# Hybrid block, one core: compact norms, softplus sums in two fp32r passes, and mixer work moved between tiles

## Chip, core and metric

One core of a Trainium2 chip (TensorE, VectorE = DVE, ScalarE = ACT, GpSimd = POOL, SyncE = SP for the loads). The metric is the device time of one execution in microseconds, median of three runs.

## What is computed

One decoder layer, x of 256 tokens by 2048 features, fp32 throughout:

```python
proj = rms_norm(x, g1) @ w_in                    # 8 groups of 512 columns, 3 x 2048 gates
o_a = hgrn2_mixer(q, f, i, g)                    # gated linear recurrence, 4 heads of 128
o_b = s5_mixer(u)                                # complex diagonal state space, then GLU
o_c = stick_breaking_mixer(q, k, v)              # q, k normed per head
merged = sum(sigmoid(gate_k) * (o_k @ w_branch[k]) for k in range(3))
x = x + merged @ w_out
x = x + (silu(up_a) * up_b) @ w_down             # up = causal conv of rms_norm(x, g2) @ w_up
```

Branch A ends in `o * rsqrt(mean(o*o))` over each head's 128 features; branch C norms q and k the same way. Branch C also needs, per head, the sum of softplus(z) over all later keys:

```python
within = cumsum(log_keep, reverse=True) - log_keep       # log_keep = -softplus(z), masked
later = cumsum(blk_tot, reverse=True) - blk_tot          # of whole key blocks of 128
w = exp(log_sigmoid(z) + within + later)
```

## The kernel before

Everything is kept with features on the 128 partitions and the 256 tokens along the row. The big products go by output tiles of 128 features: 32 tiles for the 8 groups, 48 for the gates, then GLU, branches, `w_out`, `w_up`, `w_down`. A tile of `w_in` needs 16 blocks of 128x128 weights, in two pieces of 8. fp32 precision is had from fp32r operands (one pass each) by splitting weights and activations in a high and a low part and taking three products. So each piece is loaded by SP into one of 4 `raw` buffers, ScalarE copies it to `w_hi` (L689), VectorE writes `w_lo = raw - w_hi` (L999), and TensorE uses both: in `in_piece` (L356) as three matmuls of 256 columns per block, in `piece` (L342, L344) as one of 512 and one of 256. The ring of 4 pieces is two tiles: ScalarE may overwrite a piece once TensorE has used it, and loop step n of ScalarE and VectorE makes the pieces of tile n + 2.

All the small work of the branches is hung into the `w_in` loop, by a step number n. TensorE runs `mixers(n)` after tile n, ScalarE and VectorE run `mixers(n + 1)` in step n, behind their two pieces, so that what they do there goes on beside TensorE's tile n + 1. Each engine works in order: a long step delays the pieces that stand behind it. The order is written by hand in a table, `AT`, with `TABLE_AT` for the S5 cosine tables and `STATES_AT` for the S5 states:

```python
AT = {"norm1": 7, "s5_bT": 18, "hg_vT": 15, "hg_o": 30, "hg_ss": 31, "q_ss": 35, "k_ss": 35, "sb_vT": 36,
      "z0": 39, "z1": 39, "within0": 42, "within1": 42, "sb_o": 45}
AT.update({f"lev{k}": 12 + 2 * k for k in range(LEVELS + 1)})
STATES_AT = (43, 46, 51, 54, 59, 62, 67, 70)
```

The places that matter below:

- `lev1` to `lev8`: attention of branch A by levels. VectorE writes a level's factors (L1202, L1203), TensorE waits for them.
- The split of the normed input `a_in` (L1232), 16 blocks, four in each of steps 11 to 14; `s5_input_weights`, steps 16 and 17.
- `hg_ss`, `q_ss`, `k_ss`: the sums of squares, each as two full fp32 products of `ones` (128x128) with 512 columns, so that every row of the result is the sum (L401). Then VectorE takes the mean (L1050), ScalarE Ln and Exp, VectorE one Newton step, all on 128x1024, and multiplies.
- `z0`, `z1`: logits. ScalarE copies them out and makes log(1 + exp(-|z|)), VectorE the softplus `SOFTP` and log-sigmoid (128x1536), masks both; `within0`, `within1` sum them with the triangle `lower` and `ones` as fp32 products.
- The branch stage: VectorE's `gate_product` (L1415) multiplies a bank by its gate, GpSimd's `merge` adds three of them (L1580, L1582), ScalarE and VectorE split the sum (L894, L1406) for `w_out`. Before `merge`, GpSimd issues one load of the whole residual `x1`, 2 MB (L1570).

An fp32 matmul of the program is two records in the trace. Small fp32 products whose output is a strip of 32 rows (`s5_y`) or whose input is one (`bu`) are there already.

## Time and profile before

| | |
|---|---|
| median of 3 runs | 1419.68 us (1418.05 to 1420.31) |
| the profiled execution | 1416.86 us, span 1415.2 us |
| TensorE busy | 1401.0 us, 99% of the span |
| VectorE, ScalarE, GpSimd busy | 73%, 54%, 10% |
| chain that ended last | TensorE 84%, VectorE 8%, issue 3%, ScalarE 2% |
| mean granted TensorE clock | 0.998 |
| HBM | 184 GB/s over the span |

Busy time of TensorE is the union of its records; an idle gap of it is given with what ended it. The granted clock is 1.00 at 2.4 GHz and 0.50 at 1.2 GHz.

### The profile page before, as it was taken

The numbers are of one execution on the slowest core, as the hardware profiler recorded it, in microseconds if no ns is written. First come the engines' busy times: TensorE is split into PE (matmuls) and PEld (weight loads), VectorE is DVE, ScalarE is ACT, GpSimd is POOL, SyncE is SP. The second block draws the span as 40 slices with busy tenths as digits, with TensorE's granted clock in tenths as the row PEclk, the third lists the DMA queues.
The fourth block names the chain that finished last, engine by engine and source line by source line (L and its number), as shares of the span: only waits on it lengthen the run. The fifth ranks groups of instructions, "written<-read, shape, count | busy, mean of one in ns | idle before, by whom it ended". The sixth has DMA issues, their size and how long they took to land.

```text
span 1415.2 us, 27392 instructions
## 1 busy us (share of the span) xinstructions
PE 1401.0 (99%) x9654; PEld 1291.2 (91%) x9654; DVE 1036.5 (73%) x1412; ACT 764.4 (54%) x1058; POOL 136.7 (10%) x182
## 2 busy tenths in 40 slices
...
GB/s 291 184 171 165 164 149 153 145 179 178 147 182 177 184 190 217 204 190 192 164 208 194 192 179 194 191 191 190 182 191 192 184 193 182 204 196 193 196 205 112
DMA packets 75503, 261.66 MB, mean 185 GB/s; under 512 B 8688, under 2 KB 9232, under 8 KB 75312
## 3 DMA queue, kind: packets, MB, share of 16 engines
...
HBM read 258.66 MB, written 2.10 MB: 184 GB/s over the span
## 4 chain that ended last, share of the span: by engine, by line
PE 84%; DVE 8%; issue 3%; ACT 2%; POOL 1%; DMA 1%; SPq 0%; POOLq 0%; DVEq 0%; ACTq 0%
PE bank L342 38%; PE bank L356 22%; PE bank L344 20%; DVE w_lo L999 3%; PE pair L401 2%; PE bank L367 1%; POOL merged L1580 1%; ACT w_hi L689 1%; DMA raw<-w_br 1%; POOL merged L1582 1%; DVE tmp L1023 0%; DVE a_in L1232 0%; ACT gates L699 0%; DVE proj L1023 0%; DMA x_first<-xT 0%
## 5 line engine op out<-in xcount | busy, mean ns | idle before, releaser
L999 DVE TENSOR_TENSOR w_lo<-raw,w_hi 128x1024 fp32r<-128x1024 f32 x496 | 584.7, 1191 | 311.3 <-ACT w_hi L689 307.3
L689 ACT ACTIVATE w_hi<-raw 128x1024 fp32r<-128x1024 f32 x496 | 507.8, 1030 | 413.1 <-PE bank L344 200.7
L342 PE MATMUL bank<-h,w_hi 128*128 128x512 f32 x1408 | 488.4, 390 | 0.0
L344 PE MATMUL bank<-h,w_lo 128*128 128x256 f32 x1408 | 397.1, 282 | 0.0
L356 PE MATMUL bank<-a_in,w_hi 128*128 128x256 f32 x2048 | 367.3, 283 | 5.2 <-DVE w_lo L999 5.2
L356 PEld LDWEIGHTS bank<-a_in,w_hi 128*128 128x128 f32 x2048 | 314.1, 189 | 9.9 <-issue 6.9
L342 PEld LDWEIGHTS bank<-h,w_hi 128*128 128x128 f32 x1408 | 264.2, 188 | 55.4
L356 PE MATMUL bank<-a_in,w_lo 128*128 128x256 f32 x1024 | 286.7, 280 | 0.0
L344 PEld LDWEIGHTS bank<-h,w_lo 128*128 128x128 f32 x1408 | 266.1, 189 | 0.0
L342 PE MATMUL bank<-act,w_hi 128*128 128x512 f32 x660 | 228.8, 390 | 0.0
L356 PEld LDWEIGHTS bank<-a_in,w_lo 128*128 128x128 f32 x1024 | 194.1, 190 | 0.0
L344 PE MATMUL bank<-act,w_lo 128*128 128x256 f32 x660 | 186.1, 282 | 0.0
L342 PEld LDWEIGHTS bank<-act,w_hi 128*128 128x128 f32 x660 | 123.8, 188 | 26.0
L344 PEld LDWEIGHTS bank<-act,w_lo 128*128 128x128 f32 x660 | 124.7, 189 | 0.0
L1607 POOL TENSOR_TENSOR padded<-sum_u,rstd 128x256 f32<-128x256 f32 x88 | 73.7, 838 | 413.3 <-DVE sum_u L1020 400.5
L342 PE MATMUL bank<-a_in,w_hi 128*128 128x512 f32 x256 | 89.0, 390 | 0.5 <-DVE a_in L1406 0.5
L344 PE MATMUL bank<-a_in,w_lo 128*128 128x256 f32 x256 | 72.2, 282 | 0.0
L939 ACT ACTIVATE silu<-convd 128x256 f32<-128x256 f32 x43 | 18.0, 418 | 96.0 <-DVE convd L1472 96.0
L1470 DVE SCALAR_TENSOR_TENSOR convd<-padded,taps,convd 128x256 f32<-128x256 f32 x88 | 62.7, 712 | 1.0 <-ACT convd L959 1.0
L1472 DVE SCALAR_TENSOR_TENSOR convd<-padded,taps,convd 128x256 f32<-128x256 f32 x88 | 53.9, 613 | 11.5
L342 PEld LDWEIGHTS bank<-a_in,w_hi 128*128 128x128 f32 x256 | 48.0, 188 | 10.8 <-DVE a_in L1406 0.8
L696 ACT ACTIVATE half<-bank 128x256 f32<-128x256 f32 x135 | 49.2, 364 | 3.9 <-PE bank L344 3.9
...
## 6 DMA issues: line engine op xcount, KB each, us to landing
...
```

What stands on the lines that cost most here:

```text
L342: pe.matmul(bank[b][:, :], w[:, k * P:(k + 1) * P], a.rearrange("p a t -> p (a t)"), start=first and n == 0, stop=False, skip_group_check= ...
L344: mm = pe.matmul(bank[b][:, 0:SEQ], l[:, k * P:(k + 1) * P], a[:, 0, :], start=False, stop=last and n == len(blocks) - 1, skip_group_check ...
L356: mm = pe.matmul(bank[n % BANKS][:, 0:SEQ], x[:, k * P:(k + 1) * P], src[:, PIECE * h + k, part, :], start=h == 0 and k == 0 and m == 0, s ...
L367: mm = pe.matmul(bank[b][:, 0:SEQ], x[:, k * P:(k + 1) * P], rhs(k, part), start=first and k == 0 and m == 0, stop=last and k == blocks - ...
L401: mm = pe.matmul(out_[p0:p1, c0:c1], lhsT, rhs, start=start, stop=stop, skip_group_check=True)
L689: act_e.activation(w_hi[s][:, 0:blocks * P], raw[s][:, 0:blocks * P], ACT.Copy).then_inc(hi_ready, 1)
L696: act_e.activation(half[j % 2][:, :], bank[j % BANKS][:, SEQ:2 * SEQ], ACT.Copy).then_inc(half_copied, 1)
L939: act_e.activation(silu[:, :], convd[:, (j - 3) % 4, :], ACT.Silu).then_inc(S("silu_done"), 1)
L999: ve.tensor_tensor(w_lo[s][:, w], raw[s][:, w], w_hi[s][:, w].bitcast(F32), ALU.subtract).then_inc(lo_ready, 1)
L1470: ve.scalar_tensor_tensor(c, padded[:, j % 2, 1:SEQ + 1], taps[:, t, 1:2], c, ALU.mult, ALU.add).then_inc(S("tap1"), 1)
L1472: ve.scalar_tensor_tensor(c, padded[:, j % 2, 0:SEQ], taps[:, t, 0:1], c, ALU.mult, ALU.add).then_inc(S("conv_done"), 1)
L1607: pool.tensor_tensor(padded[:, j, 2:], sum_u[:, j, :], rstd[:, :], ALU.mult).then_inc(S("up_scaled"), 1)
```

## The change

- The three norms of branch A and C go together. `ss` is 12 fp32 products that each give a strip of 32 rows (head h in rows 32h to 32h + 31) of 256 columns; mean, Ln, Exp and Newton step run once on 128x768; then `qk_rb` (8 products) and `hg_rb` (4 products) spread the row of each head over 128 rows, with `first_rows` (128x128, ones in rows 0, 32, 64, 96) as weights, and VectorE multiplies by them out of PSUM.
- `within`: ScalarE copies the masked softplus to `softp_hi` (fp32r), VectorE makes `softp_lo`, both in step 40, a tile between mask and product; TensorE takes `lower` and `ones` (now fp32r) with each of both in one pass.
- z goes from 39 to 37, within from 42 to 41, `sb_o` from 45 to 44, `s5_bT` from 18 to 20; `s5_input_weights` from steps 16 and 17 to 17 and 19; the `a_in` split is 3 blocks in each of steps 11 to 14 and 4 in step 15; the fourth S5 table from steps 55, 56, 57 (sine in 58) to 50, 51, 58 (sine in 59).
- GpSimd loads `x1` in four parts of 512 KB, one ahead of each four tiles of `merge`, each after the part before has landed; and the first add of `merge` waits for two gate products only, the second add for the third.

```diff
@@ tables
-AT = {"norm1": 7, "s5_bT": 18, "hg_vT": 15, "hg_o": 30, "hg_ss": 31, "q_ss": 35, "k_ss": 35, "sb_vT": 36,
-      "z0": 39, "z1": 39, "within0": 42, "within1": 42, "sb_o": 45}
+AT = {"norm1": 7, "s5_bT": 20, "hg_vT": 15, "hg_o": 30, "ss": 31, "sb_vT": 34, "qk_rb0": 35, "qk_rb1": 35, "hg_rb0": 39, "hg_rb1": 39,
+      "z0": 37, "z1": 37, "within0": 41, "within1": 41, "sb_o": 44}
-KINDS = (["norm1", "s5_bT"] + [f"lev{k}" for k in range(LEVELS + 1)] + ["hg_vT", "hg_o", "hg_ss", "q_ss", "k_ss", "sb_vT"]
+KINDS = (["norm1", "s5_bT"] + [f"lev{k}" for k in range(LEVELS + 1)] + ["hg_vT", "hg_o", "ss", "sb_vT", "qk_rb0", "qk_rb1", "hg_rb0", "hg_rb1"]
-TABLE_AT = [20, 24, 28, 55]
+TABLE_AT = [(20, 21, 22, 23), (24, 25, 26, 27), (28, 29, 30, 31), (50, 51, 58, 59)]
...
@@ helper
+def split_chunks(n):
+    return range(3 * (n - 11), KT if n == 15 else 3 * (n - 10))
...
@@ tiles
-ones = sb("ones", [P, P])
+ones = sb("ones", [P, P], F32R)
+first_rows = sb("first_rows", [P, P])
-lower = sb("lower", [P, P])
+lower = sb("lower", [P, P], F32R)
...
@@ tiles
+within = ExitStack()
+sb("below_within", [P, 3 * CT * SEQ + 2 * 1024], F32, within)
+softp_hi = sb("softp_hi", [P, 2 * 1024], F32R, within)
+softp_lo = sb("softp_lo", [P, 2 * 1024], F32R, within)
+within.close()
...
@@ views
+NORM_V, NORM_Y, NORM_T1 = T[2][:, 0:3 * SEQ], T[6][:, 0:3 * SEQ], T[0][:, 0:3 * SEQ]
...
@@ TensorE, mixers(n)
-for name, sem, src in (("hg_ss", None, T[1]), ("q_ss", "q_sq", T[0]), ("k_ss", "k_sq", T[1])):
-    if n == AT[name]:
-        if sem:
-            pe.wait_ge(S(sem), 1)
-        else:
-            wait_taken(pe, "hg_o")
-        fp32_product(name, [((0, P, c * 512, (c + 1) * 512), ones[:, :], src[:, c * 512:(c + 1) * 512], True, True)
-                            for c in range(2)])
+if n == AT["ss"]:
+    wait_taken(pe, "hg_o")
+    pe.wait_ge(S("q_sq"), 1)
+    pe.wait_ge(S("k_sq"), 1)
+    fp32_product("ss", [((32 * h, 32 * h + 32, c * SEQ, (c + 1) * SEQ), ones[:, 0:32].bitcast(F32), T4[src][:, h, :], True, True)
+                        for c, src in enumerate((1, 3, 4)) for h in range(HEADS)])
+for name, parts in (("qk_rb", (1, 2)), ("hg_rb", (0,))):
+    if n == AT[name + "0"]:
+        pe.wait_ge(S("norms_rstd"), 1)
+        pe.wait_ge(S("first_rows"), 1 + HEADS)
+        outs_ = [start_product(f"{name}{e}") for e in range(2)]
+        for c, part in enumerate(parts):
+            for h in range(HEADS):
+                rows = slice(32 * h, 32 * h + 32)
+                at = 512 * (h % 2) + c * SEQ
+                mm = pe.matmul(outs_[h // 2][:, at:at + SEQ], first_rows[rows, :], NORM_Y[rows, part * SEQ:(part + 1) * SEQ],
+                               start=True, stop=True, skip_group_check=True)
+                if part == parts[-1] and h % 2:
+                    mm.then_inc(product_done, 1)
-        pe.wait_ge(S("q_normed"), 1)
-        pe.wait_ge(S("k_normed"), 1)
+        pe.wait_ge(S("q_normed"), 2)
+        for e in range(2):
+            wait_taken(pe, f"qk_rb{e}")
...
@@ TensorE, mixers(n)
-pe.wait_ge(S("sb_masked"), 2 * (hh + 1))
-sp_ = tmp[:, 4:6, :].rearrange("p a b -> p (a b)")[:, 768 * hh:768 * (hh + 1)]
-ops = []
-for i in range(2):
-    ops += [((0, P, i * SEQ, (i + 1) * SEQ), lower[:, :], sp_[:, i * SEQ:(i + 1) * SEQ], True, False),
-            ((0, P, i * SEQ + P, (i + 1) * SEQ), ones[:, :], sp_[:, 512 + i * P:512 + (i + 1) * P], False, True)]
-for i in range(2):
-    ops += [((0, P, 512 + i * P, 512 + (i + 1) * P), lower[:, :], sp_[:, 512 + i * P:512 + (i + 1) * P], True, True)]
+pe.wait_ge(S("softp_lo"), hh + 1)
+parts = [x[:, 768 * hh:768 * (hh + 1)] for x in (softp_hi, softp_lo)]
+ops = [((0, P, 0, 512), lower[:, :], x[:, 0:512], e == 0, False) for e, x in enumerate(parts)]
+ops += [((0, P, i * SEQ + P, (i + 1) * SEQ), ones[:, :], x[:, 512 + i * P:512 + (i + 1) * P], False, e == 1)
+        for e, x in enumerate(parts) for i in range(2)]
+ops += [((0, P, 512, 768), lower[:, :], x[:, 512:768], e == 0, e == 1) for e, x in enumerate(parts)]
...
@@ ScalarE, mixers(n)
-if n == AT["hg_ss"] + 2:
-    act_e.wait_ge(S("hg_var"), 1)
-    run("hg_root", T[3], T[2], ACT.Ln)
-if n == AT["hg_ss"] + 3:
-    run("hg_root", T[3], T[3], ACT.Exp, scale=-0.5)
-if n == AT["q_ss"]:
+if n == AT["ss"] - 1:
-    wait_product(act_e, "hg_ss")
-    run("q_sq", T[0], flat(SQ), ACT.Square)
-    run("k_sq", T[1], flat(SK), ACT.Square)
-if n == AT["q_ss"] + 1:
-    rough_root("q", T[3], T[2])
+    wait_product(act_e, "lev8")
+    wait_taken(act_e, "lev8")
+    run("q_sq", T[3], flat(SQ), ACT.Square)
+    run("k_sq", T[4], flat(SK), ACT.Square)
+if n == AT["ss"] + 2:
+    act_e.wait_ge(S("norms_var"), 1)
+    run("norms_root", NORM_Y, NORM_V, ACT.Ln)
+if n == AT["ss"] + 3:
+    run("norms_root", NORM_Y, NORM_Y, ACT.Exp, scale=-0.5)
-    rough_root("k", T[6], T[5])
...
@@ ScalarE, mixers(n)
+if n == AT["z0"] + 3:
+    for hh in range(2):
+        act_e.wait_ge(S("sb_masked"), 2 * (hh + 1))
+        act_e.wait_ge(S("sb_ls"), 1)
+        run("softp_hi", softp_hi[:, 768 * hh:768 * (hh + 1)], SOFTP[:, 768 * hh:768 * (hh + 1)], ACT.Copy)
...
@@ ScalarE, mixers(n)
-if n == TABLE_AT[g] + 3:
+if n == TABLE_AT[g][3]:
...
@@ ScalarE, mixers(n)
-if 11 <= n < 15:
-    for k in range(4 * (n - 11), 4 * (n - 10)):
-        act_e.wait_ge(S("x_normed"), n - 10)
+if 11 <= n < 16:
+    for k in split_chunks(n):
+        act_e.wait_ge(S("x_normed"), k // 4 + 1)
...
@@ VectorE, mixers(n)
-if n == 16 or n == 17:
-    s5_input_weights(n - 16)
+if n == 17 or n == 19:
+    s5_input_weights((n - 17) // 2)
...
@@ VectorE, mixers(n)
-if 11 <= n < 15:
-    for k in range(4 * (n - 11), 4 * (n - 10)):
+if 11 <= n < 16:
+    for k in split_chunks(n):
-if n == AT["hg_ss"] + 1:
-    mean("hg_ss", T[2], 1024)
-    ve.nop().then_inc(S("hg_var"), 1)
-if n == AT["hg_ss"] + 3:
-    inverse_root("hg", T[2], T[3], T[4])
-if n == AT["hg_ss"] + 4:
+if n == AT["ss"] + 1:
+    mean("ss", NORM_V, 3 * SEQ)
+    ve.nop().then_inc(S("norms_var"), 1)
-    tt("hg_norm", flat(HG_II), flat(HG_II), T[3], ALU.mult)
+    ts("sb_gain", gain_sb[:, 0:1], gain_sb[:, 0:1], P ** -0.5, None, ALU.mult)
+if n == AT["ss"] + 4:
+    inverse_root("norms", NORM_V, NORM_Y, NORM_T1)
+if n == AT["qk_rb0"] + 1:
+    for e in range(2):
+        wait_product(ve, f"qk_rb{e}")
+        heads = slice(2 * e, 2 * e + 2)
+        rb = product(f"qk_rb{e}").rearrange("p (h c t) -> p c h t", h=2, c=2)
+        for c, x in enumerate((SQ, SK)):
+            ins = ve.scalar_tensor_tensor(x[:, heads, :], x[:, heads, :], gain_sb[:, c:c + 1], rb[:, c], ALU.mult, ALU.mult)
+            if c == 0:
+                issue(ins, "q_normed")
+            else:
+                taken(ins, f"qk_rb{e}")
+    settle(ve, "q_normed")
+    for e in range(2):
+        wait_taken(ve, f"qk_rb{e}")
+if n == AT["hg_rb0"] + 1:
+    for e in range(2):
+        wait_product(ve, f"hg_rb{e}")
+        heads = slice(2 * e, 2 * e + 2)
+        rb = product(f"hg_rb{e}").rearrange("p (h c t) -> p c h t", h=2, c=2)
+        taken(ve.tensor_tensor(HG_II[:, heads, :], HG_II[:, heads, :], rb[:, 0], ALU.mult), f"hg_rb{e}")
+    for e in range(2):
+        wait_taken(ve, f"hg_rb{e}")
+if n == AT["hg_rb0"] + 2:
-if n == AT["q_ss"] + 1:
-    mean("q_ss", T[2], 1024)
-    ve.nop().then_inc(S("q_var"), 1)
-    mean("k_ss", T[5], 1024)
-    ve.nop().then_inc(S("k_var"), 1)
-if n == AT["q_ss"] + 2:
-    inverse_root("q", T[2], T[3], T[4])
-    ts("sb_gain", gain_sb[:, 0:1], gain_sb[:, 0:1], P ** -0.5, None, ALU.mult)
-    stt("q_normed", flat(SQ), flat(SQ), gain_sb[:, 0:1], T[3], ALU.mult, ALU.mult)
-if n == AT["q_ss"] + 3:
-    inverse_root("k", T[5], T[6], T[4])
-    stt("k_normed", flat(SK), flat(SK), gain_sb[:, 1:2], T[6], ALU.mult, ALU.mult)
...
@@ VectorE, mixers(n)
+if n == AT["z0"] + 3:
+    for hh in range(2):
+        ve.wait_ge(S("softp_hi"), hh + 1)
+        part = slice(768 * hh, 768 * (hh + 1))
+        tt("softp_lo", softp_lo[:, part], SOFTP[:, part], softp_hi[:, part].bitcast(F32), ALU.subtract)
...
@@ VectorE, mixers(n)
-if n == TABLE_AT[g]:
+if n == TABLE_AT[g][0]:
-if n == TABLE_AT[g] + 1:
+if n == TABLE_AT[g][1]:
-if n == TABLE_AT[g] + 2:
+if n == TABLE_AT[g][2]:
...
@@ VectorE, outs
-ve.wait_ge(S("x1_landed"), 16)
+ve.wait_ge(S("x1_landed"), i * 16 + 16)
...
@@ GpSimd, start
+link(pool, pool.memset(first_rows[:, :], 0.0), "first_rows")
+for h in range(HEADS):
+    link(pool, pool.memset(first_rows[32 * h:32 * h + 1, :], 1.0), "first_rows")
...
@@ GpSimd, merge(i)
-pool.dma_start(x1[:, :, :], xT).then_inc(S("x1_landed"), 16)
+    if not isinstance(i, int):
+        pool.wait_ge(S("x1_landed"), i * 16)
+    tiles = slice(i * RING, (i + 1) * RING) if isinstance(i, int) else bass.ds(i * RING, RING)
+    pool.dma_start(x1[:, tiles, :], xT[:, tiles, :]).then_inc(S("x1_landed"), 16)
-        pool.wait_ge(tile_summed, i * (3 * RING) + (BR_T + 3 * j + 3))
+        pool.wait_ge(tile_summed, i * (3 * RING) + (BR_T + 3 * j + 2))
+        pool.wait_ge(tile_summed, i * (3 * RING) + (BR_T + 3 * j + 3))
```

TensorE at `within0` and `within1` (`pair` is a PSUM buffer, `tmp` holds the softplus). Before:

```order
L401 MATMUL pair1<-tmp,lower 128x256 [waits pair_taken1,sb_masked]
L401 MATMUL pair1<-tmp,ones 128x128
L401 MATMUL pair1<-tmp,lower 128x256
L401 MATMUL pair1<-tmp,ones 128x128
L401 MATMUL pair1<-tmp,lower 128x128 x2
L401 MATMUL pair0<-tmp,lower 128x256 [waits pair_taken0,sb_masked]
L401 MATMUL pair0<-tmp,ones 128x128
L401 MATMUL pair0<-tmp,lower 128x256
L401 MATMUL pair0<-tmp,ones 128x128
L401 MATMUL pair0<-tmp,lower 128x128 x2
```

With the change:

```order
L413 MATMUL pair1<-softp_hi,lower 128x512 [waits pair_taken1,softp_lo]
L413 MATMUL pair1<-softp_lo,lower 128x512
L413 MATMUL pair1<-softp_hi,ones 128x128 x2
L413 MATMUL pair1<-softp_lo,ones 128x128 x2
L413 MATMUL pair1<-softp_hi,lower 128x256
L413 MATMUL pair1<-softp_lo,lower 128x256
L413 MATMUL pair0<-softp_hi,lower 128x512 [waits pair_taken0,softp_lo]
L413 MATMUL pair0<-softp_lo,lower 128x512
L413 MATMUL pair0<-softp_hi,ones 128x128 x2
L413 MATMUL pair0<-softp_lo,ones 128x128 x2
L413 MATMUL pair0<-softp_hi,lower 128x256
L413 MATMUL pair0<-softp_lo,lower 128x256
```

Twelve fp32 products have become 16 of fp32r, half of them 128 columns wide, and they wait for `softp_lo`.

VectorE behind the logits (L1030 on 128x1536 are softplus and log-sigmoid, then come four masks; `w_lo` are the weight pieces). Before:

```order
L1030 SCALAR_TENSOR_TENSOR tmp<-tmp 128x1536 [waits sb_ln]
L1030 SCALAR_TENSOR_TENSOR tmp<-tmp 128x1536 [waits sb_sp]
L1023 TENSOR_TENSOR tmp<-tmp,upper 128x2x128 [waits sb_ls]
L1023 TENSOR_TENSOR tmp<-tmp,upper 128x256 [waits sb_masked]
L1023 TENSOR_TENSOR tmp<-tmp,upper 128x2x128 [waits sb_masked]
L1023 TENSOR_TENSOR tmp<-tmp,upper 128x256 [waits sb_masked]
L999 TENSOR_TENSOR w_lo2<-raw2,w_hi2 128x1024 [waits hi_ready,sb_masked]
L999 TENSOR_TENSOR w_lo3<-raw3,w_hi3 128x1024 [waits hi_ready]
L999 TENSOR_TENSOR w_lo0<-raw0,w_hi0 128x1024 [waits hi_ready]
L999 TENSOR_TENSOR w_lo1<-raw1,w_hi1 128x1024 [waits hi_ready]
L1274 TENSOR_TENSOR tmp<-tmp,pair1 128x768 [waits product_done]
L1274 TENSOR_TENSOR tmp<-tmp,pair0 128x768 [waits product_done]
```

With the change, from the two pieces behind the same four masks on:

```order
L1024 TENSOR_TENSOR w_lo2<-raw2,w_hi2 128x1024 [waits hi_ready,sb_masked]
L1024 TENSOR_TENSOR w_lo3<-raw3,w_hi3 128x1024 [waits hi_ready]
L1286 TENSOR_TENSOR proj0<-proj0,pair1 128x512 [waits product_done]
L1286 TENSOR_TENSOR proj0<-proj0,pair0 128x512 [waits product_done]
L1048 TENSOR_TENSOR softp_lo<-tmp,softp_hi 128x768 [waits softp_hi,pair_taken0,pair_taken1]
L1048 TENSOR_TENSOR softp_lo<-tmp,softp_hi 128x768 [waits softp_hi,softp_lo]
L1024 TENSOR_TENSOR w_lo0<-raw0,w_hi0 128x1024 [waits hi_ready,softp_lo]
L1024 TENSOR_TENSOR w_lo1<-raw1,w_hi1 128x1024 [waits hi_ready]
L1055 SCALAR_TENSOR_TENSOR proj0<-proj0,gain_hg 128x256
L1055 SCALAR_TENSOR_TENSOR proj0<-proj0,gain_hg 128x256 [waits hg_out] x3
L1024 TENSOR_TENSOR w_lo2<-raw2,w_hi2 128x1024 [waits hi_ready,hg_out]
L1024 TENSOR_TENSOR w_lo3<-raw3,w_hi3 128x1024 [waits hi_ready]
```

Behind the masks stand now two multiplies by `hg_rb`, the two halves of `softp_lo` and the four of `hg_out`, each with pieces in between.

VectorE at the fourth S5 table (`tmp<-time_f`, the products with `tmp` 128x1024 around it). Before, steps 56 and 57:

```order
L1023 TENSOR_TENSOR tmp<-tmp 128x1024
L1333 SCALAR_TENSOR_TENSOR tmp<-time_f,s5_t,tmp 128x256 [waits s5_phase]
L1333 SCALAR_TENSOR_TENSOR tmp<-time_f,s5_t,tmp 128x256 x3
L999 TENSOR_TENSOR w_lo0<-raw0,w_hi0 128x1024 [waits hi_ready]
L999 TENSOR_TENSOR w_lo1<-raw1,w_hi1 128x1024 [waits hi_ready]
L1309 TENSOR_TENSOR proj0<-proj0,gates 128x512
L1023 TENSOR_TENSOR proj0<-proj0,gates 128x512
L1023 TENSOR_TENSOR proj1<-proj0 128x512 [waits s5_unrot]
L1026 TENSOR_SCALAR tmp<-tmp 128x1024 [waits s5_phase,s5_x]
L1023 TENSOR_TENSOR tmp<-tmp 128x1024 [waits s5_phase]
L999 TENSOR_TENSOR w_lo2<-raw2,w_hi2 128x1024 [waits hi_ready,s5_phase]
L999 TENSOR_TENSOR w_lo3<-raw3,w_hi3 128x1024 [waits hi_ready]
```

With the change, steps 50 and 51:

```order
L1048 TENSOR_TENSOR tmp<-time_f,s5_t 128x1024
L1051 TENSOR_SCALAR tmp<-tmp 128x1024 [waits s5_phase]
L1024 TENSOR_TENSOR w_lo0<-raw0,w_hi0 128x1024 [waits hi_ready,s5_phase]
L1024 TENSOR_TENSOR w_lo1<-raw1,w_hi1 128x1024 [waits hi_ready]
L1355 SCALAR_TENSOR_TENSOR proj0<-proj0,skip_s5,pair0 128x256 [waits product_done]
L1048 TENSOR_TENSOR tmp<-tmp 128x1024 [waits pair_taken0]
L1373 SCALAR_TENSOR_TENSOR tmp<-time_f,s5_t,tmp 128x256 [waits s5_phase]
L1373 SCALAR_TENSOR_TENSOR tmp<-time_f,s5_t,tmp 128x256 x3
L1024 TENSOR_TENSOR w_lo2<-raw2,w_hi2 128x1024 [waits hi_ready]
```

The first three instructions of the table stand between pieces with little else there; the last two come at step 58.

## Rows read from the trace of the kernel before

**Rows 1.** The page of the profile, part 1: busy time, share of the span and instructions.

```profile
PE 1401.0 (99%) x9654; PEld 1291.2 (91%) x9654; DVE 1036.5 (73%) x1412; ACT 764.4 (54%) x1058; POOL 136.7 (10%) x182
```

**Rows 2.** Waits of TensorE: engine, line, waited for, total us, times, longest.

```profile
PE bank L356 <- DVE w_lo L999: 5.2, 2, 3.1
PE pair L401 <- DVE tmp L1203: 2.8, 2, 1.9
PE bank L382 <- DVE gated L1415: 1.4, 1, 1.4
...
PE bank L342 <- DVE a_in L1406: 0.5, 1, 0.5
```

**Rows 3.** Timeline of TensorE at the norm product hg_ss: start us, us, instruction, count.

```profile
206.24 0.28 PE L356 MATMUL bank<-a_in,w_lo 128*128 128x256 f32 x1
...
206.60 0.28 PE L356 MATMUL bank<-a_in,w_lo 128*128 128x256 f32 x1
206.71 1.88 PE L401 MATMUL pair<-tmp,ones 128*128 128x512 f32 x4
...
208.66 0.28 PE L356 MATMUL bank<-a_in,w_lo 128*128 128x256 f32 x1
```

**Rows 4.** Timeline of TensorE at s5_y0, output in strips of 32 rows.

```profile
334.01 0.28 PE L356 MATMUL bank<-a_in,w_lo 128*128 128x256 f32 x1
334.22 1.07 PE L401 MATMUL pair<-proj,s_cT 128*32 128x256 f32 x16
...
335.56 0.28 PE L356 MATMUL bank<-a_in,w_lo 128*128 128x256 f32 x1
```

**Rows 5.** Timeline of TensorE at bu0 and bu1, input in strips of 32 rows.

```profile
290.92 0.28 PE L356 MATMUL bank<-a_in,w_lo 128*128 128x256 f32 x1
...
292.54 0.28 PE L356 MATMUL bank<-a_in,w_lo 128*128 128x256 f32 x1
```

**Rows 6.** Timeline of TensorE around within0 and within1.

```profile
281.75 0.28 PE L356 MATMUL bank<-a_in,w_lo 128*128 128x256 f32 x1
...
285.62 0.28 PE L356 MATMUL bank<-a_in,w_lo 128*128 128x256 f32 x1
```

**Rows 7.** Timeline of VectorE in the early stage.

```profile
95.46 1.67 DVE L1232 SCALAR_TENSOR_TENSOR a_in<-x_first,gain_mix,a_in 128x256 fp32r<-128x256 f32 x4
...
106.39 0.87 DVE L1023 TENSOR_TENSOR proj<-proj,s_t 128x256 f32<-128x256 f32 x2
```

**Rows 8.** Timeline of VectorE before the stall at 252 us.

```profile
253.84 2.36 DVE L999 TENSOR_TENSOR w_lo<-raw,w_hi 128x1024 fp32r<-128x1024 f32 x2 [1.95 <-ACT w_hi L689]
```

**Rows 9.** Timeline of TensorE after that stall.

```profile
255.95 0.42 PE L356 MATMUL bank<-a_in,w_lo 128*128 128x256 f32 x1
...
259.15 0.31 PE L356 MATMUL bank<-a_in,w_lo 128*128 128x256 f32 x1
```

**Rows 10.** Stretches: busy us of each engine (instructions), granted clock, DMA share, GB/s.

```profile
257.00:258.00 1.00, 1.00 (x7) 1.00 (x6) 0.97 (x2) 1.00 (x2) 0.00 (x0) 0.50 1.00 393
380.00:381.00 1.00, 1.00 (x7) 1.00 (x6) 0.96 (x3) 0.00 (x0) 0.00 (x0) 0.50 0.96 373
```

**Rows 11.** Timeline of VectorE in the states' first two steps and the table between.

```profile
365.57 1.22 DVE L1023 TENSOR_TENSOR tmp<-time_f,s_t 128x1024 f32<-128x1024 f32 x1
...
375.49 1.67 DVE L1333 SCALAR_TENSOR_TENSOR tmp<-time_f,s_t,tmp 128x256 f32<-128x256 f32 x4
```

**Rows 12.** Timeline of TensorE after z1, the first tile behind it.

```profile
264.98 0.48 PE L356 MATMUL bank<-a_in,w_hi 128*128 128x256 f32 x2
```

**Rows 13.** Timeline of VectorE, the split queued behind the softplus.

```profile
282.07 4.63 DVE L999 TENSOR_TENSOR w_lo<-raw,w_hi 128x1024 fp32r<-128x1024 f32 x4
```

**Rows 14.** Timeline of ScalarE in the branch stage.

```profile
535.40 1.58 ACT L689 ACTIVATE w_hi<-raw 128x1024 fp32r<-128x1024 f32 x2 [4.52 <-DMA raw<-w_br]
```

**Rows 15.** Timeline of GpSimd in the branch stage.

```profile
525.19 0.54 POOL L1570 DMA_DIRECT2D x<-xT  x1 [479.45 <-DVE o_s L1391]
...
592.53 1.65 POOL L1580 TENSOR_TENSOR merged<-gated 128x256 f32<-128x256 f32 x1 [1.82 <-DVE gated L1415]
```

More of the change, by code:

```diff
@@ L437, in mixers @@
                     pe.wait_ge(S("x_sq_sum"), 5)
-                    fp32_product("norm1", [((0, P, 0, SEQ), ones[:, :], squares[0][:, 0, :], True, True)])
+                    fp32_product("norm1", [((0, P, 0, SEQ), ones[:, :].bitcast(F32), squares[0][:, 0, :], True, True)])
                 if n == AT["s5_bT"]:
@@ L536, in _ @@
             for _ in range(WARM):
-                pe.matmul(pair[1][:, 0:P], ones[:, :], ones[:, :], start=True, stop=True, skip_group_check=True)
+                pe.matmul(pair[1][:, 0:P], ones[:, :].bitcast(F32), ones[:, :].bitcast(F32), start=True, stop=True, skip_group_check=True)
             for q in range(2):
```

6 lines of the change are left out of this document (3 added, 3 removed).

## Prediction

> **What bounds the kernel now.** I read first the page's busy shares: TensorE is busy 1401.0 of 1415.2 us [rows 1], so time can only be won in two ways, by work taken from TensorE or by closing one of its gaps, and work on any other engine counts only where TensorE waits for it. Next the waits of TensorE: five stalls matter, 3.1 and 2.1 us for `w_lo` (listed together as 5.2), 1.9 and 0.9 us for the level factors, 1.4 us for `gated`, and 0.5 us for `a_in` [rows 2]. Then the timeline and the stretches around them: behind each of the two `w_lo` stalls the granted clock is 0.50, 1.2 GHz [rows 10]. The blocks run slower there: from 255.95 to 259.15 five blocks take 3.20 us [rows 9], where a block (two w_hi, one w_lo) takes 0.355 us at full clock, 206.24 to 206.60 [rows 3], so 1.4 us are lost, 1.6 with the part blocks at both ends. The stalls of 1.4 to 1.9 us had no such stretch.
>
> The price of a small product is read as what it inserts between two w_lo records, less one block. For `hg_ss` that is 208.66 - 206.60 - 0.355 = 1.70 us [rows 3].
>
> **Norm products.** Removed: three of 1.70 us, 5.1 us. Added: `ss`, 12 products in output strips, has 24 records of the form of `s5_y0`, whose 16 insert 335.56 - 334.01 - 0.355 = 1.20 us; its records start (1.07 - 0.38)/15 = 46 ns apart, 0.38 being one record [rows 4], so 24 of them cost 1.20 + 8 x 0.046 = 1.57 us. `qk_rb` has the form of `bu0` with `bu1`, 292.54 - 290.92 - 0.355 = 1.27 us [rows 5], and `hg_rb` half the records, 1.27 - 8 x 0.05 = 0.85 us. Together 3.7 us; saved **1.4 us**. As a bound, without any overlap of strips a 256-column record takes half of a 512-column one, 1.70/8 = 0.21 us, and 48 of them 10.2 us.
> The Trainium skill (TensorEngine Tiling, Theoretical Speedup and Key Properties) gives strips of 32 up to four times the speed, but says that a change of tiling mode drains TensorE, which speaks against three new changes of shape. By the fourfold speed alone the three would cost 10.2/4 = 2.6 us as an estimate and save 2.5; the row has the drain in it, 1.20 us where a quarter of 16 x 0.21 is 0.85, and I go by the row.
>
> **Within.** Removed: 285.62 - 281.75 - 0.355 = 3.5 us [rows 6]. Added: four fp32r products of 512 columns and four of 256 at the pace of the main loop, 0.118 us per 256 columns [rows 3], 1.42 us, and eight of 128 columns, which no row shows in fp32r. At the same pace per column they take 0.06 us each, at the pace of fp32 (3.5 us over 2048 columns) 0.22. I take 0.08, nearest the main loop since the form of operand is the same, with a little for a weight load behind half the columns: 2.06 us in all; the ends are 1.9 and 3.2. Saved **1.5 us** (0.3 to 1.6).
> The Trainium skill (TensorE: Matmul & The Clock Gate, Back-to-back issue gap) states 81 ns for a 128-column matmul in a stream with weight loads, by which the eight take 0.65 us as an estimate and the saving is the same; no run here shows it yet.
>
> **The early stalls.** VectorE works there without a pause. Three blocks of the `a_in` split fewer stand ahead of `lev1`; four take 1.67 us [rows 7], so it gains 1.2 us, more than the 0.9 of the wait. Ahead of `lev2` all 16 blocks stand as before, but `s5_input_weights(0)` is gone: two products 0.87 us [rows 7], and two of the same size behind, 1.8 us. TensorE comes 0.9 us sooner, so its wait is 1.9 + 0.9 - 1.8 = 1.0 us. Saved **1.8 us**. The last four `a_in` blocks are now made in step 15, when TensorE has begun tile 16; it asks for the last of them 15 blocks in, 5.3 us after its start, about 2 us after it is made.
>
> **The stall of 3.1 us.** VectorE's split there began after 1.95 us of waiting for ScalarE [rows 8], and ScalarE was late from the Ln and Exp of q and k with their table loads. Both are gone (one Ln and one Exp, four tiles earlier, remain). Stall and slow clock behind it, 3.1 + 1.6 us, go. What is late next: the logits move up two tiles, and `hg_rb` and `softp_lo` come behind. Count from Z = 264.98, the first tile behind `z1` [rows 12], all of which moves along with z. VectorE starts the split queued behind the masks at 282.07, four in 4.63 us [rows 13]: the first piece is ready at Z + 18.3. Before, `within` stood ahead of the tile that needs it. Now TensorE comes for tile 41 after three tiles of 5.66 us and `hg_rb`, Z + 17.8: a new wait of **0.5 us**, too short for the clock. Next on VectorE, behind two pieces (to Z + 19.4), `hg_rb` (two of 512 columns) and `softp_lo` (two of 768), 3.3 us at 1.22 us per 1024 [rows 11] and a little for their waits, end at about Z + 22.8; `softp_hi` on ScalarE, two of under 1 us, ends about a us after the masks, at Z + 18; TensorE wants `softp_lo` at Z + 24.0. One us to spare: nothing. Saved 4.7 - 0.5 = **4.2 us**.
> Ahead of `qk_rb` the Newton step on VectorE (three of 768 columns, 2.8 us by the same row) begins some 2.3 us after tile 34 (the last piece on ScalarE, then on VectorE at 1.16 us [rows 13]) and so ends 0.5 us before tile 35 does, more with the transposes between; ScalarE's Exp stands a step earlier. Nothing.
>
> **The stall of 2.1 us.** In steps 55 and 56 the fourth table put 1.22 + 0.69 and 1.22 + 1.67 us [rows 11] beside the two longest steps of the states (4 us each). In steps 50, 51 and 58 VectorE has only its pieces and one `s5_y` add. Saved 2.15 and the slow clock, 1.6 [rows 10], **3.7 us**.
>
> **Branch stage.** The load of x1, issued at 525.19 [rows 15], runs against the weights: ScalarE waited 4.52 us for `w_br` [rows 14], and TensorE then 1.4. So the first 3.1 us were covered. A quarter of the load delays by about 1.1 us, which is covered. Saved **1.4 us**. The last `merge` now has its first add (1.65 us [rows 15]) begun ahead of the third gate product: the 0.5 us for `a_in` go. Saved **0.5 us**. Issuing three more loads, 0.54 us each [rows 15], falls into GpSimd's own waits, 1.82 us or more before a first add [rows 15]; without that cover it is 1.6 us in all, on GpSimd.
> Nothing for the strip's memsets, the bitcasts, the shorter VectorE norms: VectorE and ScalarE have pauses wherever TensorE doesn't wait.
>
> **Sum.** 1.4 + 1.5 + 1.8 + 4.2 + 3.7 + 1.4 + 0.5 = 14.5 us, from the profiled execution's 1416.86 to 1402.4, span 1400.7. The median of the runs is 2.8 us above that execution; from it the sum gives **1405.2 us**.
>
> **Rivals.** (1) One stall comes back in the packed steps 39 to 41 or at `qk_rb`. For: the margins are about 1 us, and in-order ScalarE now waits for VectorE's masks and back. Against: my count has the pieces ready in time. A stall of about 2.2 us with its slow clock is 3.8 us: 1409. Chance 0.2. (2) The split x1 load or the earlier add gives nothing, since each part still meets the weights at the start of four tiles, and the fp32r products of 128 columns take the fp32 pace: 1.9 + 1.1 us, 1408. Chance 0.09. (3) The strips do not do what they are there for: `ss` and both `rb` overlap worse than `s5_y0`, up to 10.2 for 3.7 us: up to 1411.7. Against: the same form is in the trace twice. Chance 0.04. (4) Slower: in each `merge(i)` the load of GpSimd, with an address from a register and a wait for the part before, holds the adds; VectorE's gate products wait for `merged`, banks stay full, TensorE stands. Place: three loop bodies, i = 1 to 3. To lose 14.5 us and 3 more each must hold GpSimd for 5.8 us beyond its 1.8 us of cover, 7.6 against 0.54 for a fourfold larger issue: 1424 with 8.5 us each. Chance 0.03. (5) Two or more of these and several unseen waits together leave within 0.2%: chance 0.04.
>
> **Numbers.** My forecast has 0.6: 1405.2. A measurement of this kernel tells 0.2%, 2.8 us, from no change (its three runs lie 2.3 us apart). The range: below, both small waits left (1.0 and 0.5) go too and the runs fall 2 us lower, 1401.5; above, rivals 1 and 2 with some spread, and most of 3, 1412. Faster 0.93, same 0.04, slower 0.03.
>
> **What would show it.** TensorE's waits: no `w_lo` stall above 1 us and no stretch at clock 0.50, mean clock 1.000; `lev2` with 1.0 us left, `lev1` with none; `ss` inserting 1.6 us, `qk_rb` 1.3, `hg_rb` 0.85, `within` 2.1; about 0.5 us before tile 41; ScalarE's wait for `w_br` near 1 us; TensorE busy about 1395. It is wrong if a clock of 0.50 appears anywhere, if the gap count rises in the packed steps, or if `within` takes over 3 us.

## Result and profile after

| | before | after |
|---|---|---|
| median | 1418.87 us (1417.13 to 1420.31, 4 runs) | 1402.95 us (1402.88 to 1403.75, 4 runs) |
| the profiled execution | 1416.86 us, span 1415.2 | 1402.92 us, span 1401.4 |
| mean granted TensorE clock | 0.998 | 1.000 |

The changed kernel is 1.1% faster: the ratio is 0.989, with an interval of 0.9873 to 0.9907. The forecast was 1405.2 us, within 1401.5 to 1412. From span to span the gain is 13.8 us where the sum said 14.5.

Part 1 of the page of the changed kernel (the columns are those of [rows 1]):

```profile
PE 1394.3 (99%) x9682; PEld 1285.5 (92%) x9682; DVE 1030.6 (74%) x1409; ACT 754.0 (54%) x1050; POOL 143.4 (10%) x190
```

TensorE is busy 6.7 us less than in [rows 1] and idle 7.1 us less. Its waits, changed kernel (engine and tile, released by, us in total, times, longest):

```profile
PE pair L413 <- DVE tmp L1228: 1.6, 3, 1.2
PE pair L559 <- POOL ones L1585: 1.2, 1, 1.2
PE bank L354 <- DVE w_lo L1403: 0.9, 1, 0.9
PE bank L368 <- DVE w_lo L1024: 0.5, 1, 0.5
PE bank L354 <- DVE w_lo L1024: 0.2, 1, 0.2
```

Beside [rows 2]: the two long `w_lo` stalls are gone and 0.5 us is left, `lev1` no longer waits, `lev2` waits 1.2 (the longest in the first line; the other two, 0.2 and 0.25 us, stand at later levels), `gated` and `a_in` are gone. New is the third line, 0.9 us for `w_lo` in the head of the program. The second line is the start of the program, 1.1 us before. The clock, changed kernel, stretches of 100 us (busy us of each engine, then clock, DMA share, GB/s):

```profile
200.00:300.00 100.00, 99.48 (x857) 96.39 (x856) 63.89 (x73) 69.31 (x74) 0.00 (x0) 1.00 0.48 158
300.00:400.00 100.00, 100.00 (x878) 97.42 (x877) 91.07 (x114) 47.99 (x59) 0.00 (x0) 1.00 0.54 177
```

No stretch at 0.50 is left in the whole span, against [rows 10]. The small products, changed kernel, timeline of TensorE (start, us, engine, line, operation):

```profile
205.93 0.27 PE L368 MATMUL bank<-a_in,w_lo 128*128 128x256 f32 x1
206.13 1.50 PE L413 MATMUL pair<-tmp,ones 128*32 128x256 f32 x24
207.57 0.50 PE L368 MATMUL bank<-a_in,w_hi 128*128 128x256 f32 x2
207.90 0.28 PE L368 MATMUL bank<-a_in,w_lo 128*128 128x256 f32 x1
...
230.84 0.27 PE L368 MATMUL bank<-a_in,w_lo 128*128 128x256 f32 x1
231.04 1.15 PE L489 MATMUL pair<-tmp,first_rows 32*128 32x256 f32 x16
232.12 0.50 PE L368 MATMUL bank<-a_in,w_hi 128*128 128x256 f32 x2
232.46 0.28 PE L368 MATMUL bank<-a_in,w_lo 128*128 128x256 f32 x1
...
257.23 0.28 PE L368 MATMUL bank<-a_in,w_lo 128*128 128x256 f32 x1
257.44 0.71 PE L489 MATMUL pair<-tmp,first_rows 32*128 32x256 f32 x8
258.09 0.51 PE L368 MATMUL bank<-a_in,w_hi 128*128 128x256 f32 x2
258.43 0.28 PE L368 MATMUL bank<-a_in,w_lo 128*128 128x256 f32 x1
```

Between two `w_lo` records, less one block of 0.355: `ss` 1.61 us, `qk_rb` 1.27, `hg_rb` 0.85. And `within`:

```profile
270.10 0.28 PE L368 MATMUL bank<-a_in,w_lo 128*128 128x256 f32 x1
270.21 0.39 PE L413 MATMUL pair<-softp_hi,lower 128*128 128x512 f32 x1
270.44 0.40 PE L413 MATMUL pair<-softp_lo,lower 128*128 128x512 f32 x1
270.67 0.33 PE L413 MATMUL pair<-softp_hi,ones 128*128 128x128 f32 x2
270.84 0.39 PE L413 MATMUL pair<-softp_lo,ones 128*128 128x128 f32 x2
271.07 0.33 PE L413 MATMUL pair<-softp_hi,lower 128*128 128x256 f32 x1
...
272.74 0.28 PE L368 MATMUL bank<-a_in,w_lo 128*128 128x256 f32 x1
```

It inserts 2.64 - 0.355 = 2.28 us against 3.5 in [rows 6]. Four products of 128 columns run from 270.67 to 271.07, 0.10 us each.

Where the 13.8 us come from, by the first TensorE record of each stage in the two profiled executions (us):

| from, to | length before | length after | gained | forecast |
|---|---|---|---|---|
| start, `norm1` | 51.89 | 53.20 | -1.31 | 0 |
| `norm1`, `lev2` | 57.66 | 55.91 | 1.75 | 1.8 |
| `lev2`, first norm product | 97.16 | 97.02 | 0.14 | 0 |
| first norm product, `bu0` | 84.41 | 77.66 | 6.75 | 1.4 + 1.5 + 4.2 |
| `bu0`, GLU | 219.06 | 215.03 | 4.03 | 3.7 |
| GLU, `w_out` | 79.99 | 78.29 | 1.70 | 1.4 |
| `w_out`, `w_up` | 89.51 | 88.75 | 0.76 | 0.5 |
| `w_up`, end | 735.5 | 735.5 | 0.0 | 0 |

### The profile page after: what moved, and what is told of

Read it like the earlier page. It is cut to its first block, busy times and chain, and to the rows that moved or that the text cites. A ratio compares the mean times of both kernels' runs of the same rounds, so it can differ in the third digit from the quotient of the medians.

```text
span 1401.4 us, 27481 instructions
## 1 busy us (share of the span) xinstructions
PE 1394.3 (99%) x9682; PEld 1285.5 (92%) x9682; DVE 1030.6 (74%) x1409; ACT 754.0 (54%) x1050; POOL 143.4 (10%) x190
## 4 chain that ended last, share of the span: by engine, by line
PE 91%; DVE 6%; ACT 2%; DMA 1%; issue 0%; SPq 0%; ACTq 0%; DVEq 0%
PE bank L354 40%; PE bank L368 22%; PE bank L356 21%; PE bank L394 5%; DVE w_lo L1024 2%; PE pair L413 1%; PE bank L379 1%; DVE a_in L1257 0%; ACT gates L721 0%; ACT w_hi L711 0%; DMA x_first<-xT 0%; DVE tmp L1055 0%; DVE tmp L1048 0%; DVE x_first L1217 0%; ACT tmp L721 0%
## 5 line engine op out<-in xcount | busy, mean ns | idle before, releaser
L368 PE MATMUL bank<-a_in,w_hi 128*128 128x256 f32 x2048 | 363.1, 281 | 0.5 <-DVE w_lo L1024 0.5
```

Of the source, the lines that this page charges most:

```text
L368: mm = pe.matmul(bank[n % BANKS][:, 0:SEQ], x[:, k * P:(k + 1) * P], src[:, PIECE * h + k, part, :], start=h == 0 and k == 0 and m == 0, s ...
```

## Experiments

Eleven runs. Those without another word are the changed kernel with one edit. Some have one execution only; there the readings rest on the stage lengths in the trace, since the head alone moves a time by up to 1 us.

**The fourth S5 table back in its old steps.**

```diff
-TABLE_AT = [..., (50, 51, 58, 59)]
+TABLE_AT = [..., (55, 56, 57, 58)]
```

> The changed kernel with the fourth S5 table back in steps 55, 56, 57 (sine in 58); everything else stays. Theory: TensorE gets back a wait of 2.1 us for w_lo near 370 us, and behind it a stretch of some 3.2 us at a granted clock of 0.50, which costs 1.6 us more. So 3.7 us longer than the changed kernel: about 1406.7 us, and the rest of the trace as it was. Rival 1: the slow clock belonged to the two stalls together, or to the phase of the program; then only the wait comes back, 2.1 us, 1405.0 us. Rival 2: the wait was made by the order of the steps before (z and within two tiles later), and the table in 55 does no harm now: 1403.0 us.

Measured: 1406.15 us (1404.98 to 1407.35, 4 runs), 3.2 us above the changed kernel. TensorE's waits from 300 to 400 us and the stretches around, this kernel:

```profile
PE bank L368 <- DVE w_lo L1024: 2.2, 1, 2.2
```

```profile
370.00:380.00 10.00, 9.38 (x86) 8.69 (x86) 7.78 (x9) 5.53 (x6) 0.00 (x0) 1.00 0.50 160
```

The wait is back as forecast, but in this execution the clock stays at 1.00 behind it, and the span is only 2.0 us longer. The four executions have spans of 1403.4 and 1404.0 us at a mean clock of 1.000, and 1405.2 and 1405.8 at 0.999. Only the first has a profile; that the clock of 0.999 is one slow stretch behind this same wait is read from the mean clocks and spans. So the wait costs 2.2 us, and a slow clock comes in some executions and not in others, at a price of about 1.8 us by the spans (the head of the program, which varies by 1 us, is in this figure). In time the theory holds for two runs and the first rival for the other two; its reason, that the slow clock needs both stalls, does not, since there is one stall here. The second rival is out.

**The kernel before, once more, unchanged.**

> The kernel before, unchanged, for a second profile of it. Two things vary perhaps by themselves. The head: the first profile of the kernel before had no wait on TensorE between 6 and 20 us, all five of kernels with the change had 0.4 to 1.2 us there. If the change makes it, there is again none here; if the landing of x_first varies, some wait is here too. The slow clock: its runs have mean clocks from 0.999 to 0.996, where one stretch of 3.2 us at 0.50 makes 0.001; so between one and three such stretches are expected, and the span between 1415.4 and 1418.3 us follows them.

Measured: 1419.07 us, span 1417.4, clock 0.996. Timeline of TensorE, and stretches of this execution:

```profile
8.58 0.50 PE L342 MATMUL bank<-a_raw,w_hi 128*128 128x512 f32 x1 [0.38 <-DVE w_lo L1363]
10.76 0.50 PE L342 MATMUL bank<-a_raw,w_hi 128*128 128x512 f32 x1 [0.52 <-DVE w_lo L1363]
```

```profile
110.00:120.00 10.00, 9.41 (x89) 9.34 (x90) 7.77 (x11) 1.94 (x3) 0.00 (x0) 0.83 0.46 141
250.00:270.00 20.00, 16.93 (x126) 16.55 (x125) 16.05 (x15) 16.21 (x18) 0.00 (x0) 0.91 0.48 154
...
380.00:390.00 10.00, 9.13 (x70) 8.44 (x71) 8.03 (x9) 5.52 (x6) 0.00 (x0) 0.83 0.48 156
```

Two things follow. The head's stall is in the kernel before too: here `norm1` starts at 52.93, 1.04 us later than in its first profile. ScalarE waits 0.35 us for `w_in` and 0.75 us for `x_first` behind its first copies, where it waited for neither in the first profile; in the changed kernel's profile it waits 1.24 us for `x_first`. So at least 1.0 of the 1.3 us that the changed kernel lost there come without the change too. And there are three slow stretches, not two: the 1.9 us wait at `lev2` is followed by one here, and was not in the first profile. That is the 2.2 us between the two executions: 1.04 in the head and 1.41 between `lev2` and the first norm product, less 0.2 further on.

All runs of the kernel before agree: of the 17 executions with a listed clock, 2 have 0.999 (spans 1414.7 and 1415.4), 8 have 0.998 (1415.2 to 1416.3) and 7 have 0.996 (1417.2 to 1418.3). The two profiles have two and three slow stretches at 0.998 and 0.996.

**The early work back in its old steps.** Beside the lines shown, `s5_bT` is back at 18 and the loops over the blocks end with step 14.

```diff
-    return range(3 * (n - 11), KT if n == 15 else 3 * (n - 10))
+    return range(4 * (n - 11), 4 * (n - 10))
...
-if n == 17 or n == 19:
-    s5_input_weights((n - 17) // 2)
+if n == 16 or n == 17:
+    s5_input_weights(n - 16)
```

> The changed kernel with the early work where it was: four a_in blocks in each of steps 11 to 14, s5_input_weights in steps 16 and 17, s5_bT at 18. Theory: the waits for lev1 (0.9 us) and lev2 (1.9 us) come back in place of 1.2 us, so that lev8 starts 1.7 us later than in the changed kernel, counted from the end of the stage on unnormed input, and the run is 1404.6 us. Rival: the 1.2 us that the changed kernel still waits at lev2 have another cause than the queue of VectorE, and lev2 stays at about 1.2 with lev1 back: 0.9 us longer. Of the head: the changed kernel lost 1.1 us before 20 us (a wait for x_first by ScalarE, then 0.9 us on TensorE). If this is how a transfer happened to land, this run may have it or not; if it is the five memsets that GpSimd does first, it has it again.

Measured: 1405.94 us, span 1404.3. TensorE's waits from 85 to 130 us, and the stretch behind, this kernel:

```profile
PE pair L413 <- DVE tmp L1228: 2.9, 2, 1.9
```

```profile
110.00:120.00 10.00, 9.68 (x92) 9.56 (x93) 7.51 (x12) 2.17 (x3) 0.00 (x0) 0.83 0.43 138
```

The two waits in the line are 0.99 us at `lev1` and 1.92 at `lev2`. Counted from `norm1`, it falls behind the changed kernel by 1.05 us at `lev1` and by 0.78 more at `lev2`: 1.83, the forecast 1.8. Behind the 1.9 us wait stands a slow stretch once more, worth 1.4 us, which no theory had in its sum. The rest is head (0.6 us better here) and pace (below). The theory of the queue holds.

**GpSimd's five memsets later.** The memsets of `first_rows` go behind the time index.

> The changed kernel with the five memsets of first_rows moved behind the time index in GpSimd's start, so that its first microseconds are those of the kernel before. Theory: the head's loss (0.4 to 1.2 us on TensorE ahead of 12 us) is how the first transfers land, and stays in this range: 1402.9 us with 1 us either way. Rival: the memsets disturb the head (writes of GpSimd against transfers or against VectorE); then TensorE waits for nothing between 6 and 20 us, and the run gains some 1.0 us: 1401.9.

Measured: 1403.57 us, span 1402.0, `norm1` at 52.97, waits of 0.64 and 0.79 us in the head. The first microseconds are those of the kernel before here, and the waits are there all the same, with 1.03 us of ScalarE for `x_first`. With the second profile of the kernel before, which has no such memsets and waits too, the memsets are out. `norm1` starts between 52.27 and 53.20 us in all profiles of this study but the very first, the kernel before at 51.89.

**Within as fp32 again.** Products of the unsplit softplus with `lower` and `ones`, `softp_hi` and `softp_lo` left out.

> The changed kernel with within0 and within1 as fp32 products of the unsplit softplus again, at the same place, and without softp_hi and softp_lo. Theory: within inserts 3.5 us in place of 2.3, TensorE's wait of 0.5 us ahead of tile 41 stays since it hangs on the masks, and no other wait comes: 1.2 us longer, 1404.1 us. Rival: the split costs more than its own product time, since ScalarE and VectorE do 3.3 us more in step 40; then the 0.5 us go as well and the loss is only 0.7 us, 1403.6.

Measured: 1404.54 us, span 1403.0. `bu0` comes 1.21 us later than in the changed kernel (285.00 for 283.79), with `norm1` at the same time, and the 0.5 us wait stays. The theory holds: the split itself costs TensorE nothing. Another 0.4 us came with the pace, below.

**x1 in one load again**, ahead of `merge(0)`.

> The changed kernel with x1 loaded by one transfer of 2 MB ahead of the first merge, while the first add of each merge still begins after two gate products. Theory: the load runs against w_br again, ScalarE waits some 4.5 us for it and TensorE 1.4 us for w_lo or gated: 1404.4 us. Rival: it was the earlier first add that took the wait for gated away, not the split of the load; then ScalarE waits but TensorE doesn't, 1403.0 us, and in the trace TensorE has no wait in the branch stage.

Measured: 1404.74 us (1403.67 to 1405.01, 4 runs). Waits of ScalarE and TensorE from 510 to 600 us, this kernel:

```profile
ACT w_hi L711 <- DMA raw<-w_br: 3.8, 1, 3.8
...
PE bank L394 <- DVE gated L1455: 0.7, 1, 0.7
```

The stage from GLU to `w_out` is 1.44 us longer, as the theory had it; but the wait is only 0.7. The tile at the wait and the next one lose another 0.25 us, and 0.5 us is pace: a tile of four blocks took 1.40 us ahead of the wait (524.38 minus 522.98) and 1.413 in the 35 tiles behind it; the changed kernel keeps 1.40 throughout. The rival is out: TensorE waits again though the first add is early.

**The first add of merge late again.**

```diff
-pool.wait_ge(tile_summed, i * (3 * RING) + (BR_T + 3 * j + 2))
+pool.wait_ge(tile_summed, i * (3 * RING) + (BR_T + 3 * j + 3))
```

> The changed kernel with the first add of each merge again held until all three gate products are there; x1 stays in four parts. Theory: a wait of 0.5 us for a_in comes back at the start of w_out, and nothing else: 1403.4 us. Rival: with the split load of x1 the adds aren't late even so, or the slower first add (1.1 us against 0.85) was the only thing won or lost: no wait, 1402.9. In the run with x1 in one load, TensorE waited 0.7 us and not 1.4 for gated; if the adds were the other half of that, a wait in the branch stage of up to 0.7 us shows here, 1404.0.

Measured: 1403.75 us, span 1402.2. TensorE's waits from 560 to 680 us:

```profile
PE bank L354 <- DVE a_in L1446: 0.5, 1, 0.5
```

From `w_out` to `w_up` it takes 0.76 us more, and GLU to `w_out` is unchanged. The theory holds, with 0.3 us more than the wait. The two edits of the branch stage act apart: one on `gated`, one on `a_in`.

**The products of ss in another order.**

```diff
-for c, src in enumerate((1, 3, 4)) for h in range(HEADS)
+for h in range(HEADS) for c, src in enumerate((1, 3, 4))
```

> The changed kernel with the 12 products of ss in another order: the three sources of one head behind each other (strip 0 three times, then strip 1, and so on) in place of four strips in turn. Theory: strips overlap only where neighbours use different ones, so that at each strip six records run one after the other at 0.21 us or so (half of a 512 column record, 1.70 us over 8): 24 x 0.21 = 5 us less what overlaps at the three changes of strip, in place of 1.6: 1406 us. Rival: order doesn't matter, since the records start 46 ns apart in any case: 1.6 us, 1402.9 us.

Measured: 1404.18 us, span 1402.6. Timeline of TensorE:

```profile
205.61 2.87 PE L413 MATMUL pair<-tmp,ones 128*32 128x256 f32 x24
208.41 0.50 PE L368 MATMUL bank<-a_in,w_hi 128*128 128x256 f32 x2
```

Neither: 1.37 us more, not 3.4 and not 0. The record starts are (2.87 - 0.38)/23 = 0.108 us apart, against (1.50 - 0.38)/23 = 0.049 with the strips in turn. The order is worth a factor of 2.2. Six records of one strip in a row do not take 0.21 us each, half of a record of 512 columns, so the bound from which I priced the third rival was about twice too high even with this order. Why, no run tells.

**Logits back at 39.** With `hg_rb` 41, within 43, `sb_o` 46; the compact norms stay.

> The changed kernel with the logits back at 39 and all behind them two later as well (hg_rb 41, within 43, sb_o 46), so that the compact norms alone stand against the stall of 3.1 us. Theory: that stall came from the Ln and Exp of q and k with their table loads; they are gone, so it doesn't come back and 0.5 us stay ahead of tile 43. But VectorE now has the subtraction of within and the rotation of bu0 in step 43, and the masks of w with the scans in step 44, some 5.9 and 5.8 us beside its pieces, more than two tiles give: a new wait of about 0.5 us near tile 46: 1403.4 us. Rival: the move of z by two tiles, not the norms, took the stall away: 3 us are back, with a slow clock or without, 1406 to 1407.5 us.

Measured: 1411.05 us, span 1409.5, clock 0.998. TensorE's waits from 250 to 330 us:

```profile
PE pair L539 <- DVE tmp L1314: 4.7, 1, 4.7
PE bank L368 <- DVE w_lo L1024: 0.5, 1, 0.5
```

The question is answered: the stall of 3.1 us does not come back with z, 0.5 us stays. So the compact norms took it away, and not the move of z. Which part of them did it is read from the kernel before. Timeline of ScalarE, kernel before:

```profile
239.81 1.06 ACT L699 ACTIVATE tmp<-tmp 128x1024 f32<-128x1024 f32 x1 [4.88 <-DVEq L1247]
...
250.66 1.07 ACT L699 ACTIVATE tmp<-tmp 128x1024 f32<-128x1024 f32 x1
...
252.69 1.99 ACT L689 ACTIVATE w_hi<-raw 128x1024 fp32r<-128x1024 f32 x2
```

The first line is an Ln that waited for VectorE's mean; from there on ScalarE is busy without a pause, with the Ln and Exp of q and k and four table loads of 1.28 us among the pieces, and makes the late pieces at 252.69. No run takes the Ln and Exp away alone.

The rest of the expectation is wrong. With the step that the split puts between mask and product, z at 39 brings `within` to step 43 (the kernel before has it at 42), where `bu0` stands. `bu0` needs the two `pair` buffers that `within` has filled, and VectorE takes them (L1314) only behind pieces, `softp_lo` and the outputs of branch A: 4.7 us of waiting, and a slow clock, which here begins within the wait. Stretches, this kernel:

```profile
285.00:290.00 5.00, 1.12 (x12) 1.06 (x16) 3.73 (x4) 1.19 (x1) 0.00 (x0) 0.81 0.76 238
290.00:295.00 5.00, 5.00 (x31) 4.35 (x24) 3.78 (x6) 1.58 (x2) 0.00 (x0) 0.51 0.14 57
```

I had counted VectorE's load and missed the buffer. So the norms remove the stall, and with `softp_lo` a step later, z and `within` have to come earlier to keep the buffers free for `bu0`.

**The changed kernel again, and a faster one.** The second moves `s5_input_gain`, `s5_input_weights` and, in VectorE's program, `sb_ls`; `s5_bT` goes from 20 to 22:

```diff
-if n == 15:
+if n == 17:
     s5_input_gain()
-if n == 17 or n == 19:
-    s5_input_weights((n - 17) // 2)
+if n == 19 or n == 21:
+    s5_input_weights((n - 19) // 2)
...
+if n == AT["z0"] + 3:
+    stt("sb_ls", Z, Z, 0.0, LOG1P, ALU.min, ALU.subtract)
 if n == AT["hg_rb0"] + 1:
...
     stt("sb_sp", SOFTP, Z, 0.0, LOG1P, ALU.max, ALU.add)
-    stt("sb_ls", Z, Z, 0.0, LOG1P, ALU.min, ALU.subtract)
     causal("sb_masked", SOFTP)
```

> The changed kernel, unchanged, beside the next one on the same chip. Its granted clock is 1.000 in every execution, since its longest wait behind 20 us is 1.2 us, and its runs lie within about 1 us of each other, where those of the kernel before lie 3 us apart: 1402.9 to 1403.9 us.

> The changed kernel with its two remaining waits of the w_in stage taken on: s5_input_gain (15 small operations of VectorE, 3.2 us) from step 15 to 17, s5_input_weights to steps 19 and 21, s5_bT to 22; and the log-sigmoid of VectorE (sb_ls, 1.8 us) from before the masks to the step behind, ahead of the multiply by hg_rb, so that the two weight pieces are split 1.8 us sooner. Theory: both waits hang on VectorE's queue alone: the 1.2 us at lev2 and the 0.5 us ahead of tile 41 go, 1.7 us, and softp_lo, now made behind sb_ls, is still in time: 1401.3 us. Rival: softp_hi waits for sb_ls and comes 1.8 us later, softp_lo with it, and TensorE waits about 0.5 to 1 us at within: only the 1.2 us at lev2 are won, 1401.9 us or a little more.

Measured on one chip: the changed kernel 1402.91 us (1402.58 to 1403.48), clock 1.000 four times; the new one 1401.66 us (1401.55 to 1402.01). Each has four runs, which don't overlap; against the kernel before the new one has a ratio of 0.9882 (0.9865 to 0.9898). Its waits of TensorE:

```profile
PE pair L559 <- POOL ones L1586: 1.2, 1, 1.2
PE bank L354 <- DVE w_lo L1404: 0.4, 1, 0.4
PE pair L413 <- DVE tmp L1228: 0.3, 1, 0.3
PE pair L413 <- DVE proj L1332: 0.2, 1, 0.2
PE bank L354 <- DVE w_lo L1024: 0.2, 1, 0.2
```

Both waits are gone. From `norm1` to `lev2` it takes 1.6 us less than the second profile of the changed kernel (whose waits there are 0.2 and 1.3), of which 0.3 go back as a wait at a later level; between `hg_rb` and `bu0` it gains 0.7. Of this, 0.4 go back at `sb_o`: it stands a tile behind `bu0` and waits 0.24 us for `pair`, since VectorE reaches `bu0`'s products a little later relative to TensorE. `softp_lo` was in time, by 0.7 us. Between the medians lie 1.25 us of the 1.7 forecast; the two edits were not run apart, their shares are read from the trace.

## Why the prediction was right, and where it was off

- **What bounds the kernel.** Right: every gain came from TensorE's own work, its waits or its clock, and each wait named went or shrank as said.
- **Norm products.** 1.61 + 1.27 + 0.85 = 3.73 us measured for 3.7. The row of `s5_y0` was the right price: it has the strips in turn, and whatever a change of shape costs. The fourfold speed of the Trainium skill (TensorEngine Tiling, Theoretical Speedup and Key Properties) alone would have said 2.6 as an estimate. The Trainium skill says there too (Key Properties) that different tiles of the array can work in parallel, and the run with the other order agrees: records start 49 ns apart where neighbours are in different strips, 108 ns where three products of one strip stand together. What the change of shape costs by itself, no run shows.
- **Within.** The step that was mis-sized is "I take 0.08": 128 columns of fp32r took 0.10 us each, 0.80 for 0.64, the 512 and 256 columns 1.48 us for 1.42. In all 2.28 us, so 1.2 saved and not 1.5. The Trainium skill (TensorE: Matmul & The Clock Gate, Back-to-back issue gap) has 81 ns for a matmul of 128 columns in a stream with weight loads; the eight took 0.80 us where that makes 0.65 as an estimate, so the measurement stands.
- **Early stalls.** 1.75 us for 1.8, and the undo gave 1.83. `lev1` has no wait, `lev2` 1.2 for 1.0.
- **Stall of 3.1 us.** The run with z at 39 shows that the compact norms removed it; that it was ScalarE's Ln and Exp fits the trace and is not shown alone. The new wait is 0.5 us at the tile named. The count from Z was 0.2 us off: Z + 18.3 forecast for the first piece, TensorE started on it at 264.53 - 246.06 = Z + 18.5. `softp_lo` was ready at Z + 22.7 for 22.8 and wanted at Z + 24.2 for 24.0. That bu0's buffers depend on the place of `within` was not seen; the change had it right, so it cost the forecast nothing.
- **Stall of 2.1 us.** The wait cost what was said. The 1.6 us for the slow clock was treated as a part of each such stall. It is one in some executions only. Both profiles of the kernel before had it, so that it counted here in full was right for this execution and not for every one.
- **Branch stage.** 1.44 and 0.76 us by the two undos, for 1.4 and 0.5. In the table the first is 1.70: beside the wait of 1.45, the tile at it and the next one had lost 0.24 us before. ScalarE does not wait for `w_br` at all, where 1 us was forecast, so a quarter of the load is hidden fully.
- **The head.** Taken as equal; it was 1.3 us worse in the one execution compared. With `within`'s 0.3 this is more than the 0.7 us that are missing from 14.5; pace (0.4 us from `bu0` to GLU, which the second profile of the changed kernel does not have) and the larger gains of the branch stage go the other way. That the sum comes so close is in part luck.
- **From execution to median.** This is where the 2.2 us between 1405.2 and 1402.95 lie. I added the 2.8 us between the profiled execution and the median of before, as if they belonged to the measurement. The runs behind that median have no listed clock, but two of the three took 1419.68 and 1420.31 us, and among the 17 executions above only those at 0.996 took more than 1418 us (1418.9 to 1420.0). So it was most likely the third slow stretch, and the head. A kernel without the stalls has no such stretch: its profiled execution is its median, 1402.92 and 1402.95. From the profiled execution alone the sum gave 1402.4.
- **Rivals.** None happened. The first was near in kind: with z back at 39 such a stall comes, 4.7 us at `bu0` with its slow clock. The third was priced too high, by the run with the other order. In the fourth, 8.5 us a load less 1.8 of cover, three times, make 1425 and not 1424.
